# Two query blocks of a head side by side in the attention product, with V as the stationary operand, and narrower score products

## What is computed

```python
def _dilated_branch(q, k, v, window, dilation):      # 3 patterns (128,1), (512,4), (2048,16)
    ...
    scores = jnp.where(valid, scores, NEG_INF)
    lse = jax.nn.logsumexp(scores, axis=-1)
    p = jnp.exp(scores - lse[..., None])
    o = jnp.einsum('bnrhqk,bnkrhd->bnqrhd', p, vv)

def reference(x, ...):
    for layer in range(DEPTH):                       # 2
        proj = _rmsnorm(x, gain) @ w_in              # q, k, v: 8 heads of 64; conv_in: 1024
        q, k = _rope(_rmsnorm(q)), _rope(_rmsnorm(k))
        attn = _dilated_attention(q, k, v)           # branches weighted by their softmax denominators
        u = silu(_layernorm(_causal_dwconv(a * sigmoid(g), width 31)))
        x = x + concat([attn, u]) @ w_out
        up = _causal_dwconv(_rmsnorm(x) @ w_up, width 3)
        x = x + (silu(gate) * val) @ w_down
```

## Time and profile before

| | |
|---|---|
| Median of 3 runs (lowest to highest) | 2439.71 us (2439.69 to 2440.56) |
| The profiled execution: its own time, and its span from first to last instruction | 2438.82 us, 2437.0 us |
| PE busy, share of the span | 2406.3 us, 99% |
| DVE, ACT, POOL busy | 1578.7 us (65%), 792.1 us (33%), 154.1 us (6%) |
| Mean granted TensorE clock | 0.999 of full speed |
| Attention stages | about 251 to 397 us and 1460 to 1607 us |
| `attend`, two records for each fp32 matmul | 1152 matmul records, 4.8% of the chain that ended last |

### The profile page before, as it was taken

The page is one execution under the profiler, slowest core; times in us unless marked ns, Lnnn a source line. Parts: engine busy times, 40 slices in busy tenths (PEclk is TensorE's granted clock), DMA queues, the critical chain, the costliest instruction groups (busy, mean ns, idle before and its releaser), DMA issues.

```text
span 2437.0 us, 30435 instructions
## 1 busy us (share of the span) xinstructions
PE 2406.3 (99%) x11608; PEld 2000.4 (82%) x11608; DVE 1578.7 (65%) x1511; ACT 792.1 (33%) x1050; POOL 154.1 (6%) x57
## 2 busy tenths in 40 slices
PE   7999999999999999999999999999999999999999
PEld 6888898888888888888778888988888888888887
DVE  5999885665555555555749998846555655555555
ACT  4322674432222222222332227744322222222221
POOL 0221001100000000000103110011000000000000
PEclk9999999999999999999999999999999999999999
DMA  4324540112111111111112254301211111111111
GB/s 157 89 80 121 124 92 12 49 51 62 35 52 52 52 43 52 43 52 43 43 35 79 78 147 104 79 18 46 67 49 47 37 49 52 52 46 49 45 50 69
DMA packets 45521, 152.37 MB, mean 63 GB/s; under 512 B 7296, under 2 KB 8960, under 8 KB 45440
## 3 DMA queue, kind: packets, MB, share of 16 engines
q1 hardware_dynamic: 44576, 148.88, 21.0%
q10 hardware_dynamic: 864, 2.36, 0.2%
HBM read 129.97 MB, written 21.23 MB: 62 GB/s over the span
## 4 chain that ended last, share of the span: by engine, by line
PE 91%; issue 4%; DVE 3%; ACT 1%; POOLq 0%; DMA 0%; DVEq 0%; POOL 0%; SPq 0%; ACTq 0%
PE mm L416 59%; PE aux L416 20%; PE aux L564 5%; PE mm L528 3%; PE aux L548 3%; PE aux L443 1%; DVE y L1078 1%; PE aux L452 0%; DMA x<-xT 0%; POOLq L1380 0%; DVE x_lo L1020 0%; PE aux L509 0%; DVE w_lo L1008 0%; DVE x_lo L1215 0%; DVE o L1127 0%
## 5 line engine op out<-in xcount | busy, mean ns | idle before, releaser
L416 PE MATMUL mm<-x_hi,w_hi 128*128 128x512 f32 x1952 | 609.3, 393 | 16.1 <-DVE x_lo L1020 11.5
L416 PE MATMUL mm<-x_hi,w_lo 128*128 128x512 f32 x1952 | 604.8, 391 | 0.0
L416 PE MATMUL mm<-x_lo,w_hi 128*128 128x512 f32 x1952 | 604.1, 391 | 0.0
L416 PEld LDWEIGHTS mm<-x_hi,w_hi 128*128 128x128 f32 x1952 | 364.0, 188 | 95.4 <-issue 11.5
L416 PEld LDWEIGHTS mm<-x_lo,w_hi 128*128 128x128 f32 x1952 | 367.0, 188 | 79.5
L416 PEld LDWEIGHTS mm<-x_hi,w_lo 128*128 128x128 f32 x1952 | 366.9, 188 | 79.0
L704 ACT ACTIVATE w_hi<-w_raw 128x1024 fp32r<-128x1024 f32 x154 | 161.9, 1058 | 656.0 <-PE mm L416 458.1
L1078 DVE SCALAR_TENSOR_TENSOR y<-u_pad,cpar,y 128x1024 f32<-128x1024 f32 x240 | 314.0, 1341 | 3.4 <-ACT y L757 2.6
L1014 DVE TENSOR_TENSOR x<-x,aux 128x1024 f32<-128x1024 f32 x176 | 214.7, 1220 | 121.3 <-PE aux L416 110.8
L1008 DVE TENSOR_TENSOR w_lo<-w_raw,w_hi 128x1024 fp32r<-128x1024 f32 x154 | 192.5, 1255 | 54.9 <-ACT w_hi L704 51.1
L1026 DVE TENSOR_TENSOR uv<-mm,rinv 128x1024 f32<-128x1024 f32 x44 | 53.9, 1225 | 220.1 <-PE mm L416 219.9
(11 more groups left out here) (173 smaller groups left out, 3000.6 us busy)
## 6 DMA issues: line engine op xcount, KB each, us to landing
w_raw<-weights SPq DMA_DIRECT2D x188, 512.0 KB, 3.6
qk_scratch<-m SPq DMA_DIRECT2D x64, 128.0 KB, 2.1
qk_scratch<-o SPq DMA_DIRECT2D x64, 128.0 KB, 2.1
x_hi<-qk_scratch SPq DMA_DIRECT2D x32, 256.0 KB, 6.3
q_first<-qk_scratch SPq DMA_DIRECT2D x8, 512.0 KB, 5.0
k_hh_first<-qk_scratch SPq DMA_DIRECT2D x16, 256.0 KB, 6.3
k_ll_first<-qk_scratch SPq DMA_DIRECT2D x16, 256.0 KB, 6.9
x_hi<-qk_scratch SPq DMA_DIRECT2D x8, 512.0 KB, 4.6
```

Of the source, the lines that this page charges most:

```text
L416: last = pe.matmul(acc[:, cols], a, b[:, cols], start=start and n == 0, stop=stop and n == 2)
```

## The change

`attend` is turned round and is done for two query blocks 2p and 2p + 1 at once. V's 64 columns are now the stationary operand and the transposed probabilities, 128 columns, the moving one; the even block's output goes to partitions 0 to 63 and the odd block's to 64 to 127 of the same 128 PSUM columns, with the matmuls of the two alternating. There are four such products a head (`ATTENDS`, as steps after the head's first and pair: pair 0 at s5, pair 3 at s6, pairs 1 and 2 at s1 and s2 of the next head) instead of eight. The output of a head is now transposed (channels on partitions), so ACT copies its bank to SBUF (`move_out`, step 8h + 11, after `exps`), PE transposes its four blocks back (an "h" fill, step 8h + 12, behind the turn of that step), and DVE's `read_out` reads that from `stat_b` at step 8h + 12 and then drains before it frees the bank. `BLOCKS` becomes (0, 6, 1, 7, 2, 4, 3, 5); the "o" fills move to s7 and s1 (`O_AT` 23); the stage has one step more. The transposed probabilities of even steps use the space of `cos` and the turned outputs that of `sin`, so layer 0 loads both tables again at its end, ahead of the weights of unit 24 on SP's queue. The score products of blocks 2 and 6 are 384 and 896 keys wide instead of 512 and 1024.

```diff
-O_AT = 22
-BLOCKS = (0, 7, 1, 6, 2, 5, 3, 4)
+O_AT = 23
+BLOCKS = (0, 6, 1, 7, 2, 4, 3, 5)
+ATTENDS = ((5, 0), (6, 3), (9, 1), (10, 2))
+LAST_STEP = STEPS + 10
...
+        if n >= 12 and (n - 12) % TB == 0 and n < STEPS + 12:
+            fills.append((n, "h", (n - 12) // TB, None, None))
...
+        pT_large = sb("pT_large", [P, 2 * TB, P], to=attn)
+        pT_small = cos[:].rearrange("p (k q) -> p k q", q=P)
+        o_turned = [sin[:, i * BANK:(i + 1) * BANK] for i in range(2)]
...
+                if l < DEPTH - 1:
+                    sp.wait_ge(step_done, at(l, 4 * HEADS, 4 * HEADS))
+                    sp.wait_ge(o_read, at(l, HEADS, HEADS + 2))
+                    load_rope()
...
-                    keys = (qb // 2 + 1) * 2 * P
+                    keys = max(qb + 1, 6 if qb == 4 else 2) * P
...
+                    elif kind == "h":
+
+                        pe.wait_ge(o_moved, at(l, HEADS, which + 1))
+                        blocks = [o_turned[which % 2][:, i * P:(i + 1) * P] for i in range(4)]
...
-                def attend(n):
+                def attend(h, k):
...
-                    out = stat_s[:, hh * BANK + qb * HEAD_DIM:hh * BANK + (qb + 1) * HEAD_DIM]
-                    for kb in range(qb + 1):
-                        last = pe.matmul(out, pT[n % 2][:, kb, :], vp[b][:, kb, hh * HEAD_DIM:(hh + 1) * HEAD_DIM],
-                                         start=kb == 0, stop=kb == qb)
+                    cols = slice(hh * BANK + pair * P, hh * BANK + (pair + 1) * P)
+                    for kb in range(2 * pair + 2):
+                        for half in range(2):
+                            if kb <= 2 * pair + half:
+                                last = pe.matmul(stat_s[half * HEAD_DIM:(half + 1) * HEAD_DIM, cols],
+                                                 vp[b][:, kb, hh * HEAD_DIM:(hh + 1) * HEAD_DIM],
+                                                 pT(h * TB + BLOCKS.index(2 * pair + half))[:, kb, :],
+                                                 start=kb == 0, stop=kb == 2 * pair + half)
                     last.then_inc(step_done, 1)
...
+                def move_out(h):
+
+                    act.wait_ge(step_done, at(l, 4 * HEADS, 4 * h + 4))
+                    act.wait_ge(o_read, at(l, HEADS, h + 1))
+                    act.activation(o_turned[h % 2], stat_s[:, h % 2 * BANK:(h % 2 + 1) * BANK], ACT.Copy
+                                   ).then_inc(o_moved, 1)
...
                     if n < STEPS:
                         exps(n)
+                    if n >= 11 and (n - 11) % TB == 0:
+                        move_out((n - 11) // TB)
...
-                    hh = h % 2
-                    dve.wait_ge(step_done, at(l, STEPS, (h + 1) * TB))
+                    hh, f = h % 2, [fill[1:3] for fill in FILLS].index(("h", h))
+                    dve.wait_ge(pt_full, at(l, PT, f + 1))
                     dve.reciprocal(row_rec, row_sum[:, hh, :])
                     dve.drain()
                     dve.tensor_tensor(o_nat[:, :, hh * HEAD_DIM:(hh + 1) * HEAD_DIM],
-                                      stat_s[:, hh * BANK:(hh + 1) * BANK].rearrange("p (b c) -> p b c", b=TB),
+                                      stat_b[:, f % 2 * BANK:(f % 2 + 1) * BANK].rearrange("p (b c) -> p b c", b=TB),
                                       row_rec.unsqueeze(2).broadcast_to([P, TB, HEAD_DIM]),
                                       ALU.mult).then_inc(o_read, 1)
+                    dve.drain().then_inc(pt_read[f % 2], 1)
```

More of the change, by code:

```diff
@@ L123, in turn_schedule @@
     fills = []
-    for n in range(STEPS + 9):
+    for n in range(LAST_STEP):
         if 2 <= n < STEPS + 2:
@@ L309, in raw_count, with pT @@
             return (l * (UNITS // 2) + i * (step // 2) + (base // 2 + 1)) * 16
+        def pT(n):
+            buf, qb = (pT_small, pT_large)[n % 2], BLOCKS[n % TB]
+            first = qb if qb % 2 else 0
+            return buf[:, first:first + qb + 1, :]
         def plain(eng):
@@ L362, in load_head, with load_rope @@
                         sp.dma_start(k_ll[b][half, :].bitcast(F32), rows(1, 1)).then_inc(head_loaded[b], 16)
+                def load_rope():
+                    for table, dst in enumerate((sin, cos)):
+                        for h in range(HPT):
+                            sp.dma_start(dst[h * HALF:(h + 1) * HALF, :].rearrange("f (c q) -> f c q", c=HPT),
+                                         rope_scratch[table].rearrange("c f q -> f c q")).then_inc(rope_loaded, 16)
                 if l:
@@ L577, in out_part @@
                         last.then_inc(mm_full, 1)
-                for n in range(STEPS + 9):
-                    if n == STEPS + 2:
+                for n in range(LAST_STEP):
+                    if n == STEPS + 3:
                         pe.wait_ge(o_split, at(l, 2 * PAIRS, 2 * PAIRS - 2))
-                    if n in (STEPS + 2, STEPS + 3):
-                        out_part(0, 0, [n - STEPS - 2], 0)
+                        out_part(0, 0, [0], 0)
+                    if n == STEPS + 5:
+                        out_part(0, 0, [1], 0)
                     if n < STEPS:
@@ L589, in _ @@
                     for f in range(PT):
-                        if FILLS[f][0] == n and FILLS[f][1] == "p":
+                        if FILLS[f][0] == n and FILLS[f][1] in "ph":
                             turn(f)
-                    if 3 <= n < STEPS + 3:
-                        attend(n - 3)
+                    for k, (at_step, _) in enumerate(ATTENDS):
+                        if (n - at_step) % TB == 0 and 0 <= n - at_step < STEPS:
+                            attend((n - at_step) // TB, k)
                     for f in range(PT):
@@ L844, in read_turn @@
                     if kind == "p":
-                        if which == 0:
+                        if which == 1:
                             act.wait_ge(qk_stored, at(l, QK_STORES, QK_STORES + 16))
-                        if which >= 2:
-                            act.wait_ge(step_done, at(l, STEPS, which - 1))
-                        act.activation(pT[which % 2][:, a:z, :], bank[:, 0:(z - a) * P].rearrange(
+                        if which >= 4:
+                            act.wait_ge(step_done, at(l, 4 * HEADS, which // 4 * 2 - 1 + which % 2))
+                        act.activation(pT(which)[:, a:z, :], bank[:, 0:(z - a) * P].rearrange(
                             "p (k q) -> p k q", q=P), ACT.Copy).then_inc(pt_read[f % 2], 1)
@@ L1241, in _ @@
                             read_turn(f)
-                    if n >= 11 and (n - 11) % TB == 0:
-                        read_out((n - 11) // TB)
+                    if n >= 12 and (n - 12) % TB == 0:
+                        read_out((n - 12) // TB)
                 def out_add(u, parts=range(2)):
```

22 lines of the change are left out of this document (11 added, 11 removed).

## The result

The changed kernel takes **2471.36 us** (median; 2470.87 to 2471.90) against 2439.70 for the kernel before on the same chip: ratio 1.0131, 95% interval 1.0113 to 1.0148. It is slower, as forecast, but by 31.7 us and not by 11. The profiled execution has a span of 2469.1 us.

What follows compares the result with a forecast made beforehand. PE bounds attention, DVE close behind. Head intervals sum to 125.4 for 123.85 us; with tail, start and changes of width +5.5 a layer, +11: 2438.8 + 11 = 2449.8, plus 0.9 for the median: 2451 us. Range 2428 to 2484.

Steps and rivals of the forecast that it cites:

- The clock (0.08): Rival, chance 0.08: PE's wait behind output-turn heads halves its clock, some 2 us more of the path, six times: 2465 us.
- head with output turn: Attention head during which the output is turned, three of seven intervals: DVE decides, 20.9 us, or 21.2 with changes of width.
- Going between full-width and half-width matmuls: PE, attention stage: each change free or 0.16 us, taken as 0.08; 40 counted a layer, +3.2 us a layer.
- plain head: Attention head without an output turn: a round of PE's queue and waits, 16.4 us, or 17.0 with changes of width.
- The first interval, 14.7: First head interval of a layer: no turned head, 13.8 us of DVE's own work and 0.9 of waits.
- The tail, +0.9: End of the attention stage: copy, four turns and read-out one behind another, partly covered by the output projection, +0.9 us.
- a slot of two matmuls costs 0.215: Attention product on PE: two half-width matmuls run at once, 0.215 us a slot, 20 slots a head, 4.3 us for 8.1.
- the first rival: Attention product: the halves do not overlap, a slot with two matmuls costs 0.43 us, 2489 us; chance 0.14.
- the two `x_lo` waits: DVE in a head with output turn: first `x_lo` waits 0.93 us, second 2.26 us, behind the exp of 896 keys.
- The second rival: Attention product: the moving side is cheaper, a slot costs 0.113 us, 2429 us; chance 0.16.
- the third: Rival: waits in the heads are 0.7 us a head shorter than chained, so gain and new waits cancel, 2440 us; chance 0.20.
- Reloading the tables: SP's queue at the end of layer 0: goes unseen; without cover, eight DMAs delay a weight load by a few us.

Runs made afterwards that it cites:

- e1: Changed kernel with the next step's scores computed two more times on PE ahead of the wait for ACT's copy, results overwritten; 2457.75 us.
- e3: Changed kernel with the output turns one step later, at s0 and s2 (`O_AT` 24, one step more); 2464.07 us.
- e5: Changed kernel with ACT's copy of the turned bank first in its step, ahead of the probability copies and the exp; 2443.67 us.
- e9: e7 with two overwritten matmuls more ahead of each product, full width then half width, adding no change of width; 2449.52 us.
- e10: e7 with the same two added matmuls as e9 in the other order, adding two changes of width a product; 2479.46 us.
- e11: e7 with pair 0 right ahead of pair 3 and pair 1 right ahead of pair 2, four changes of width fewer a head; 2434.78 us.
- e7: Changed kernel with the changes of e5 and e3 together, and DVE's read-out ahead of the tap of its step; 2432.92 us.
- e2: Changed kernel with the product's halves one after the other: all of the even block first, then all of the odd; 2496.86 us.

## Why the prediction was right and wrong

The direction, and most of the chain of waits, were right; the size was not.

- **The step that failed is "The clock (0.08)".** I had the mechanism and its price: a fall behind each head with output turn, about 2 us of the path, six times over (six times 2 is 2463 us; the 2465 stated is 2 too much). I left it out of the sum because I knew half pace only from a stop of 11 us at the kernel's start. The runs show it at all six places (2.05 to 2.55 us each) and once more behind 1.79 us of idle time: 14.8 us. The last wait was 2.63 us, or 1.65 ahead of a tail, and PE then worked at half pace for some 5 us, not 6. Every kernel that shortens the idle time or fills it (e1, e3, e5) takes some or nearly all of the falls away. Without them the changed kernel would stand near 2456.6, 6 us above the forecast.
- **Going between full-width and half-width matmuls** was mis-sized: 0.08 taken as a compromise between nothing and 0.16; e9 and e10 give 0.13 to 0.17. A plain head then comes to 16.4 + 8 x 0.13 = 17.4, and 17.5 was measured where the clock held. With 40 a layer it is some 4 us in all. The upper end, the time that a turn stays beyond its pace, was the better guess. e11, with four changes fewer a head, did not bring their price back, so not all of them are on the path in e7.
- **The first interval, 14.7,** was wrong: I let DVE decide it, with 0.9 us of waits. It took 16.5 in every version with the halves alternating and no matmuls added to the product, 3 us in all. In e7's trace DVE still waits 1.10 and 1.07 us for PE's scores in it, so PE's queue sets it, as in a plain head.
- **The tail, +0.9,** was too short. As built it was 4.4 in layer 0: 2.55 by the clock, 1.06 by a copy that comes late (e1's 21.14 against e5's 20.08), and 0.8 for the rest. In layer 1, whose tail was 20.81 before, it was 2.9 with the clock and 0.3 without.
- **Right:** that a slot of two matmuls costs 0.215. The four products of a plain head with the clock at 1.00 took 0.58, 1.02, 1.46 and 1.90 us to the next start for 2, 4, 6 and 8 slots: 0.22 a slot and 0.14 for leaving the half width (timeline of PE):

```profile
1505.62 0.66 PE L591 MATMUL aux<-cos,sa 128*64 128x128 f32 x6
1506.20 0.73 PE L548 MATMUL mm<-x_hi 128*128 128x512 f32 x2
...
1507.19 1.97 PE L591 MATMUL aux<-pT_large,sa 128*64 128x128 f32 x30
1509.09 0.96 PE L548 MATMUL mm<-x_hi 128*128 128x512 f32 x4
...
1513.24 1.09 PE L591 MATMUL aux<-cos,sa 128*64 128x128 f32 x14
1514.26 0.39 PE L548 MATMUL mm<-k_hh_first,q_first 128*128 128x256 f32 x1
...
1514.81 1.53 PE L591 MATMUL aux<-pT_large,sa 128*64 128x128 f32 x22
1516.27 0.50 PE L548 MATMUL mm<-k_hh_first,q_first 128*128 128x512 f32 x1
```

  Also right: that the halves overlap, against the first rival (a kernel without the overlap, e2, is 25.5 us slower than the changed one); PE's idle time ahead of `sin`; the two `x_lo` waits, in the timeline of DVE:

```profile
305.49 0.69 DVE L1255 TENSOR_TENSOR x_lo<-rinv,x_hi 128x512 fp32r<-128x512 f32 x1 [0.87 <-ACT rinv L886]
...
311.16 0.70 DVE L1255 TENSOR_TENSOR x_lo<-rinv,x_hi 128x512 fp32r<-128x512 f32 x1 [2.17 <-ACT rinv L886]
```

  0.87 and 2.17 where 0.93 and 2.26 stood, and 21.36 for a head with output turn where 21.2 did.
- **The second rival** (a cheaper moving side) is out by the same 0.22 a slot, **the third** (shorter waits) by the 21.36.
- Reloading the tables was costed at nothing. No run took it out alone, but e7, which still reloads them, is faster than the kernel before.

What stays open is which idle times lead to a fall. The 1.79 us did so once of eight times in the changed kernel and six of eight in e2, whose waits are the same; the 1.65 us ahead of the tail did so both times in the changed kernel and never in e2; the 2.79 us of e3 once of four; and one fall is left in e5. One execution of each kernel was profiled.

## What to carry to other kernels

Where a change takes work off the busiest engine and leaves a new wait in its place, price the wait twice: its length, and the half pace of TensorE that can follow, since here idle times of 1.65 to 2.63 us cost 1.4 to 2.55 us more on the next 3 to 6 us of full work, at seven of fourteen such waits. A copy that TensorE waits for goes to the head of its engine's step, not behind an exp of 1.15 us: that order alone was worth 27.7 of 31.7 us. Where a product needs another width than its neighbours, count the changes of width at about 0.15 us each, against what the overlap of the halves saves; and expect less than that back from removing some (e11).

## What the runs showed of the hardware

- Two matmuls of 64 columns side by side run at once if issued alternately: 0.063 us a record in the changed kernel against 0.10 in e2, where one half follows the other. A lone half-width matmul costs next to nothing beside the other half (e9, starts 0.02 us apart).
- The page "TensorE: Matmul & The Clock Gate" of the Trainium skill, Part 3, lets a weight load overlap matmuls in flight only when the row group differs. The halves share all rows, and their overlap in the changed kernel (0.063 us a record against e2's 0.10) speaks against taking that as a bar here.
- A change between full and half width costs TensorE 0.13 to 0.17 us (e9, e10).
- In the changed kernel the granted clock fell to 0.50 at all four waits of 2.63 us, at one of eight of 1.79, and at the 1.65 us ahead of each tail, and stayed there while TensorE was busy again, for 3 to 6 us. The same waits in e2, and 2.79 us in e3, gave falls at other places and not at others.
- Extra matmuls in the idle stretch shortened the kernel by 13.6 us (e1).
